# Column strips for the group norm of an SSM layer and for the query norm of an attention layer, with a wait put before some GpSimd splits

## The reference

```python
y = x * lax.rsqrt(jnp.mean(x * x, axis=-1, keepdims=True) + EPS)     # rmsnorm, of queries too (over 128)
y = y.reshape(b, L, D_INNER) * jax.nn.silu(z.astype(jnp.float32))
yg = y.reshape(b, L, SSM_GROUPS, D_INNER // SSM_GROUPS)
yg = yg * lax.rsqrt(jnp.mean(yg * yg, axis=-1, keepdims=True) + EPS) # the SSM norm
y = (yg.reshape(b, L, D_INNER) * norm_w.astype(jnp.float32)).astype(u.dtype)
return y @ w_out, new_conv, final.astype(u.dtype)
```

## Time and profile before

| | us |
|---|---|
| median of the runs (lowest to highest) | 1044.82 (1044.59 to 1044.83) |
| the profiled execution's own time | 1044.69 |
| its span, first to last instruction | 1042.9 |
| mean granted clock of TensorE | 0.990 of full speed |
| busy: PE, DVE, ACT, POOL | 994.5, 591.4, 462.8, 365.2 |

### The profile page before, as it was taken

The page is one execution under the profiler, slowest core; times in us unless marked ns, Lnnn a source line. Parts: engine busy times, 40 slices in busy tenths (PEclk is TensorE's granted clock), DMA queues, the critical chain, the costliest instruction groups (busy, mean ns, idle before and its releaser), DMA issues.

```text
span 1042.9 us, 18690 instructions
## 1 busy us (share of the span) xinstructions
PE 994.5 (95%) x7448; PEld 917.9 (88%) x7448; DVE 591.4 (57%) x1433; ACT 462.8 (44%) x811; POOL 365.2 (35%) x275
## 2 busy tenths in 40 slices
PE   8999999999999999999997899999999999999988
PEld 7998899979999799987996879998889987998867
DVE  5115431264214442255686587976879667896773
ACT  5324623257124633157535336343553436525553
POOL 4241133113332242311824144442354343542700
PEclk9999999999999999999999899999999999999989
DMA  6342121251232222200333643427242372426303
GB/s 195 103 149 84 56 84 50 59 180 41 82 107 100 81 82 84 85 21 1 85 104 117 167 136 92 149 60 221 76 154 82 104 205 61 136 82 190 108 11 97
DMA packets 144118, 106.37 MB, mean 102 GB/s; under 512 B 10258, under 2 KB 135364, under 8 KB 143840
## 3 DMA queue, kind: packets, MB, share of 16 engines
q1 hardware_dynamic: 115032, 92.24, 28.3%
q10 hardware_dynamic: 29000, 12.94, 4.8%
HBM read 92.44 MB, written 16.79 MB: 105 GB/s over the span
## 4 chain that ended last, share of the span: by engine, by line
PE 75%; DVE 14%; issue 4%; ACT 3%; POOL 2%; DMA 1%; ACTq 0%; SPq 0%; DVEq 0%; POOLq 0%
PE pp L1190 18%; PE pp L1192 17%; PE pp L1191 17%; DVE cv L1892 2%; PE pS L1294 2%; PE pS L1520 2%; PE pT_ L1499 1%; PE pO L1513 1%; PE pO L1509 1%; PE pO L1269 1%; DVE z L2034 1%; PE pO L1460 1%; ACT sm L792 1%; POOL w_lo_raw L603 1%; PE pO L1340 1%
## 5 line engine op out<-in xcount | busy, mean ns | idle before, releaser
L603 POOL TENSOR_TENSOR w_lo_buf<-w_raw_buf,w_hi_buf 128x512 fp32r<-128x512 f32 x214 | 287.6, 1375 | 522.2 <-ACT w_hi_buf L684 416.8
L1190 PE MATMUL pp<-h_hi,w_hi_buf 128*128 128x280 f32 (+1 forms) x1248 | 380.3, 305 | 5.7 <-DVE rb L1866 2.6
L1192 PE MATMUL pp<-h_hi,w_lo_buf 128*128 128x280 f32 (+1 forms) x1248 | 364.1, 292 | 0.0
L1191 PE MATMUL pp<-h_lo,w_hi_buf 128*128 128x280 f32 (+1 forms) x1248 | 363.5, 291 | 0.0
L1190 PEld LDWEIGHTS pp<-h_hi,w_hi_buf 128*128 128x128 f32 x1248 | 236.4, 189 | 16.8 <-issue 9.3
L1191 PEld LDWEIGHTS pp<-h_lo,w_hi_buf 128*128 128x128 f32 x1248 | 236.3, 189 | 4.6 <-issue 4.1
L1192 PEld LDWEIGHTS pp<-h_hi,w_lo_buf 128*128 128x128 f32 x1248 | 236.3, 189 | 0.0
L684 ACT ACTIVATE w_hi_buf<-w_raw_buf 128x2048 fp32r<-128x2048 f32 (+1 forms) x55 | 104.0, 1892 | 37.2 <-DMA w_raw_buf<-in_w_attn_in 16.0
L1678 DVE TENSOR_TENSOR x<-x,pp 128x272 f32<-128x272 f32 (+3 forms) x128 | 56.3, 440 | 79.2 <-PE pp L1192 78.4
L1190 PE MATMUL pp<-og_hi,w_hi_buf 128*128 128x280 f32 (+2 forms) x256 | 75.5, 295 | 2.5 <-DVE x L1678 1.3
L1192 PE MATMUL pp<-og_hi,w_lo_buf 128*128 128x280 f32 (+2 forms) x256 | 74.5, 291 | 0.0
(11 more groups left out here) (322 smaller groups left out, 1764.6 us busy)
## 6 DMA issues: line engine op xcount, KB each, us to landing
w_raw_buf<-in_w_attn_in SPq DMA_DIRECT2D x16, 1024.0 KB, 5.2
w_raw_buf<-in_w_ssm_in SPq DMA_DIRECT2D x16, 1024.0 KB, 5.5
w_raw_buf<-in_w_attn_out SPq DMA_DIRECT2D x8, 1024.0 KB, 6.3
s_in<-in_state_ssm SPq DMA_DIRECT2D x32, 256.0 KB, 4.2
out<-s_in SPq DMA_DIRECT2D x32, 256.0 KB, 3.1
seg<-a_scratch ACTq DMA_DIRECT2D x16, 512.0 KB, 4.3
w_raw_buf<-in_w_ssm_out SPq DMA_DIRECT2D x8, 1024.0 KB, 5.4
w_raw_buf<-in_w_attn_in SPq DMA_DIRECT2D x8, 512.0 KB, 6.3
```

The source lines that it names most:

```text
L603: ins = pool.tensor_tensor(low_buf(n)[:, piece], raw[n % RAW_SLOTS][:, piece], high_buf(n)[:, piece].bitcast(F32), ALU.subtract)
L1190: pe.matmul(dst, hi[:, k, cols], a_hi[:, k, tk], start=(k == 0), stop=False)
L1191: pe.matmul(dst, hi[:, k, cols], a_lo[:, k, tk], start=False, stop=False)
L1192: mm = pe.matmul(dst, lo[:, k, cols], a_hi[:, k, tk], start=False, stop=(k == depth - 1))
```

## The change

Three edits.

1. The query sums of all four heads are done in one place, after gate half (0, 0). Four matmuls with 32 weight columns each give the sample tokens' sums. For the prompt, ones[:, 0:32] are the weights and the squares are moved, one head to each strip of 32 output rows, in two halves of 280 columns. ACT takes the logarithm of the result (128 by 560) into `sq[0]`, PE turns it by five transposes (`turn_logs`, behind `scores(s, 0)`), and ACT takes Exp of every 32nd column. Two further square buffers are the key norm's `ksq` and `rk`.
2. In SSM groups 0 to 2 the sum over channels becomes `strips_y` (four matmuls into four strips of 32 rows of one bank), a copy of the strips by ACT, and `total_y` (one matmul with 128 by 128 ones; every strip holds its sum 32 times, hence the scale 1/(32 WIDTH)). `total_y` stands behind a half of a projection, and the final state's transposes move behind x half (1, 0).
3. POOL waits in the slab that follows gate (kv of the next group, or out of group 3): before its first piece until `soft_max` of unit 3 is done, before its third until that of unit 4 is.

```diff
-        sq = [at(f"sq{i}", [P, T]) for i in range(2)]
+        sq = [at(f"sq{i}", [P, T]) for i in range(2)] + [ksq, rk]
...
+                        if n in beside_soft and c in (0, m // 2):
+                            pool.wait_ge(soft_a, UNITS * beside_soft[n] + (5 if c else 4))
                         ins = pool.tensor_tensor(low_buf(n)[:, piece], raw[n % RAW_SLOTS][:, piece],
...
-                if 4 * s + h >= 2:
-                    act.wait_ge(ssq_done, 4 * s + h - 1)
-                act.activation(sq[h % 2][:, :], q[:, h, :], ACT.Square).then_inc(sq_ready, 1)
+                if h == 3:
+                    act.wait_ge(k_ready, s + 1)
+                act.activation(sq[h][:, :], q[:, h, :], ACT.Square).then_inc(sq_ready, 1)
...
-                act.wait_ge(ssq_done, 4 * s + 4)
-                link(act.activation(crow[:, 0:21], misc[:, 0:21], ACT.Ln, bias=eps[:, 1:2]))
-                act.activation(crow[:, 0:21], crow[:, 0:21], ACT.Exp, scale=-0.5).then_inc(c_ready, 1)
+                act.wait_ge(ssq_done, 2 * s + 1)
+                link(act.activation(crow[:, 20:21], misc[:, 16:17], ACT.Ln, bias=eps[:, 1:2]))
+                act.activation(crow[:, 20:21], crow[:, 20:21], ACT.Exp, scale=-0.5).then_inc(c_ready, 1)
+                act.wait_ge(ssq_done, 2 * s + 2)
+                act.activation(sq[0][:, :].rearrange("p (h t) -> p h t", h=2), pT_[:, :, 0:HALF], ACT.Ln,
+                               bias=eps[:, 1:2]).then_inc(logs_ready, 1)
+                act.wait_ge(turned, s + 1)
+                act.activation(crow[:, 0:20].rearrange("p (c h) -> p c h", h=HEADS),
+                               fT[:, 0:640].rearrange("p (c h r) -> p c h r", h=HEADS, r=32)[:, :, :, 0],
+                               ACT.Exp, scale=-0.5).then_inc(c_ready, 1)
...
+                    if g + 1 < GROUPS:
+                        act.wait_ge(strips_done, 2 * g + part + 1)
+                        act.activation(xc[:, 0, tk], pS[:, part, 0:n], ACT.Copy).then_inc(strips_ready, 1)
+                        act.wait_ge(ssy_done, 2 * g + part + 1)
+                        link(act.activation(v, pS[:, 1, 0:n], ACT.Ln, bias=eps[:, 0:1], scale=1.0 / (32 * WIDTH)))
...
+            def sum_q(s):
+
+                pe.wait_ge(sq_ready, 4 * s + 4)
+                if s:
+                    pe.wait_ge(o_ready, UNITS * s)
+                for h in range(HEADS):
+                    mm = pe.matmul(misc[32 * h:32 * h + 32, 16:17], sq[h][:, PROMPT:T], ones[:, 0:1],
+                                   start=True, stop=True)
+                mm.then_inc(ssq_done, 1)
+                pe.wait_ge(tok_ready, s + 1)
+                for half in range(2):
+                    for h in range(HEADS):
+                        mm = pe.matmul(pT_[32 * h:32 * h + 32, half, 0:HALF], ones[:, 0:32],
+                                       sq[h][:, half * HALF:(half + 1) * HALF], start=True, stop=True)
+                mm.then_inc(ssq_done, 1)
+
+            def turn_logs(s):
+
+                pe.wait_ge(logs_ready, s + 1)
+                for i, c in enumerate((1, 2, 3, 4, 0)):
+                    mm = pe.transpose(fT[:, i * P:(i + 1) * P], sq[0][:, COL[c]:COL[c] + P], ident)
+                mm.then_inc(turned, 1)
...
-                sum_q(s, 0)
                 tile_of("q", s, 2)
-                sum_q(s, 1)
                 tile_of("q", s, 3)
-                sum_q(s, 2)
                 project("gate", s, 0, 0)
-                sum_q(s, 3)
+                sum_q(s)
                 scores(s, 0)
+                turn_logs(s)
                 project("gate", s, 0, 1)
...
+            def strips_y(g, part):
+                tk = part_of(g, part)
+                pe.wait_ge(xw_done, UNITS * (g + 1))
+                if part:
+                    pe.wait_ge(rg_ready, 2 * g + 1)
+                pe.wait_ge(sqy_ready, 8 * g + 4 * part + HEADS)
+                for t in range(HEADS):
+                    mm = pe.matmul(pS[32 * t:32 * t + 32, part, 0:tk.stop - tk.start], ones[:, 0:32], xc[:, t, tk],
+                                   start=True, stop=True)
+                mm.then_inc(strips_done, 1)
+
+            def total_y(g, part):
+                tk = part_of(g, part)
+                pe.wait_ge(strips_ready, 2 * g + part + 1)
+                pe.matmul(pS[:, 1, 0:tk.stop - tk.start], ones[:, :], xc[:, 0, tk],
+                          start=True, stop=True).then_inc(ssy_done, 1)
...
                 project("x", s, 0, 0)
                 if g:
-                    sum_y(g - 1, 1)
+                    strips_y(g - 1, 1)
                 project("x", s, 0, 1)
                 if g:
+                    total_y(g - 1, 1)
+                project("x", s, 1, 0)
+                if g:
                     final_state(g - 1)
-                tile_of("x", s, 1)
+                project("x", s, 1, 1)
...
-                    sum_y(g, 0)
+                    strips_y(g, 0)
                     project("bc", s + 1, 1, 1)
+                    total_y(g, 0)
```

More of the change, by code:

```diff
@@ L361, in build @@
         sq_ready, ssq_done, c_ready = sem("sq_ready"), sem("ssq_done"), sem("c_ready")
+        logs_ready, turned = sem("logs_ready"), sem("turned")
+        strips_done, strips_ready = sem("strips_done"), sem("strips_ready")
         s_done, soft_a, exp_done, p_ready = sem("s_done"), sem("soft_a"), sem("exp_done"), sem("p_ready")
@@ L417, in colsum @@
         def colsum(c):
-            return 16 if c == 5 else 17 if c == 0 else (c - 1) * 4
+            return 20 if c == 5 else 16 if c == 0 else (c - 1) * 4
         def fill_pairs(g):
@@ L591, in _ @@
             done = [0]
+            beside_soft = {slab_no[("kv", s + 1, 0)] if s + 1 < GROUPS else slab_no[("out", s, 0)]: s
+                           for s in range(GROUPS)}
             def split_lo(upto):
@@ L1112, in scale_y @@
                 def scale_y(part):
-                    act.wait_ge(ssy_done, 2 * g + part + 1)
                     tk = part_of(g, part)
                     v, n = scale_of(g)[:, tk], tk.stop - tk.start
-                    link(act.activation(v, pS[:, part, 0:n], ACT.Ln, bias=eps[:, 0:1], scale=1.0 / WIDTH))
+                    if g + 1 < GROUPS:
[3 more added lines that the diff above has]
+                        link(act.activation(v, pS[:, 1, 0:n], ACT.Ln, bias=eps[:, 0:1], scale=1.0 / (32 * WIDTH)))
+                    else:
+                        act.wait_ge(ssy_done, 2 * g + part + 1)
+                        link(act.activation(v, pS[:, part, 0:n], ACT.Ln, bias=eps[:, 0:1], scale=1.0 / WIDTH))
                     act.activation(v, v, ACT.Exp, scale=-0.5).then_inc(rg_ready, 1)
@@ L1288, in scores @@
                         pe.matmul(pS[:, i, :], lhs, kcT[:, 4 * i:4 * i + 4, :], start=True, stop=True)
-                    pe.wait_ge(c_ready, s + 1)
+                    pe.wait_ge(c_ready, 2 * s + 1)
                     pe.matmul(misc[:, 32:64], lhs, kq[:, PROMPT:T], start=True, stop=True).then_inc(s_done, 1)
@@ L1304, in transposes @@
                 if u == 0:
-                    pe.wait_ge(tok_ready, s + 1)
+                    pe.wait_ge(c_ready, 2 * s + 2)
                 p = sm[v % 2]
@@ L1537, in _ @@
                 if g:
-                    pe.wait_ge(rg_ready, 2 * g - 1)
+                    pe.wait_ge(strips_ready, 2 * g - 1)
                 else:
@@ L1692, in soft_max @@
                 dve.wait_ge(s_done, v + 1)
-                dve.wait_ge(c_ready, s + 1)
+                dve.wait_ge(c_ready, 2 * s + (2 if u else 1))
                 if v >= 2:
```

## The result

| | us |
|---|---|
| kernel after, median of four runs (lowest to highest) | 1029.7 (1028.3 to 1031.7) |
| kernel before, in the same comparison | 1044.7 (1043.9 to 1044.8) |
| ratio after to before, 95% interval | 0.9859 (0.9838 to 0.9881) |
| profiled execution of after, its span | 1028.36, 1026.6 |

The gain is 15 us by the medians and 16.3 us between the two profiled executions (1044.69 to 1028.36); 18.9 was forecast. The median lies in the range, but two of the three edits brought more than forecast and the third lost where a small gain was forecast.

The account below looks back on a forecast made before the run. PE carries 75% of the chain of waits, DVE 14%. Savings of 6.8 (GpSimd pieces), 9.3 and 1.3 (query sums, groups 1 to 3 and 0) and 1.5 (SSM norm) sum to 18.9 us, from 1044.69 to 1025.8; range 1021 to 1032.5.

Parts of the forecast that it names:

- the 1.7 to 1.9 us of PE's waiting: Softmax unit 3, each attention group: of 3.1 us DVE time saved, 1.7 to 1.9 are PE's; 6.8 us in four groups.
- margin of tenths: Moved GpSimd pieces: first two end near 100.4, `normalise` starts at about 100.6; both fits have a few tenths to spare.
- rival A: Softmax units 3 and 4: moved pieces collide with `normalise` again, gaining 2.4 instead of 6.8 us; 1030.2 us, chance 0.10.
- 0.94 + 0.24 + 0.3: Query sums' added PE work: 0.94 us two stripped halves of 280 columns, 0.24 loads and gaps, 0.3 one-column sample passes.
- Rival B: Query sums and SSM norm: strips do not run abreast with 280 or 384 columns; 1041.8 us, chance 0.04.
- The wait for gate's remainder (0.4): Attention group 0: PE reaches the gate slab before POOL's remainder is done, costing 0.4 us of the query-sum saving.
- the clock: Group 0, after PE's longer stall: TensorE may stay longer at its lower clock, worth 0 to 1.5 us.
- Part 0: SSM norm, first part: strips and total save 1.0 us of PE, but PE then waits 0.9 before x half (0, 0).
- the 0.90 us for GpSimd: SSM boundary: PE arrives early at x half (0, 0) and waits 0.9 us for POOL's remainder of slab x0.
- rival D: SSM boundaries: output slabs load late behind the moved final state, PE waits beyond 5.0 us slack; 1048.6 us, chance 0.03.
- Rival C: SSM stretch: DVE-POOL contention hits other instructions, 1 us a boundary, and clock costs 1.5 in group 0; 1031.8 us, chance 0.10.

Follow-up runs that it names:

- pieces_only: Only the GpSimd waits before two pieces of the slab that follows gate, on the kernel before: 1037.07 us, ratio 0.9925.
- one_gate: `pieces_only` with one GpSimd wait in place of two, so all four pieces start after unit 3's maxima: 1039.61 us, ratio 0.9945.
- query_only: Only the query sums in strips, done in one place, on the kernel before: 1033.57 us, ratio 0.9894.
- norm_only: Only the SSM norm by strips, copy and total, with the final state one half later, on the kernel before: 1050.85 us, ratio 1.0055.
- no_norm: Query sums in strips and the GpSimd waits together, without the SSM norm change, on the kernel before: 1025.12 us, ratio 0.9804.
- load_gate: Full change plus first output slab loaded before the final-state wait, and GpSimd waiting before the second until y part 0's remainders are done: 1021.79 us.
- move_only: `no_norm` with only the final state's transposes moved behind x half (1, 0), sums staying four full matmuls: 1037.40 us, ratio 0.9937.

## Why the prediction was right, and where it was wrong

**Edit 3, right in mechanism, somewhat small.** 6.8 us forecast, 7.6 by the end of attention in `pieces_only` and 8.2 by the medians. The step was the 1.7 to 1.9 us of PE's waiting a group, of which I took the lower end; it was 1.9. The margin of tenths was real (pieces end 0.1 us after `normalise` begins), and rival A, which lives on it, did not come. Of its two collisions one was forced in `one_gate`: 2.5 us by the medians, 1.6 by the end of attention, where A had 4.4 for both, so its price was about right. But it had the small instructions held, and what was held is the four multiplications. That the excess of `pieces_only` over 7.6 is real is not shown.

**Edit 1, the sum mis-sized.** 3.1 us a group forecast, 3.6 measured, so the added work cost 5.24 - 3.6 = 1.6 us of PE instead of 2.13. The rows say where: from the first one-column pass to the scores it is 72.02 - 70.87 = 1.15 us, for which I had 0.94 + 0.24 + 0.3 = 1.48. The one-column passes in strips cost about 0.1, not 0.3 (less than the 0.2 that I had as the least), and of the 0.24 for loads and gaps only 0.1 shows. The five transposes cost 0.50 (2.46 us from the scores to the next half of gate in after, 1.96 before), for which I had 0.55 + 0.1. Rival B is dead: the strips run abreast at 280 and at 384 columns (0.85 us, 0.9 forecast), and the drain that the Trainium skill (TensorEngine Tiling, Key Properties) warns of does not show beside these times. Group 0 was forecast to keep 1.3; in `query_only` GpSimd's split of unit 3 comes 2.1 us earlier (93.90 against 95.97), which is about 3.6 - 1.36 with nothing off. The wait for gate's remainder (0.4) did not come, and the clock cost nothing more: PE's stall grows from 1.61 to 2.82 us, as worked out, but the low clock behind it lasts no longer. The rows are `query_only` and then before; the stretch from 52 to 54 was not in the earlier trace rows.

```profile
52.00:54.00 2.00, 1.09 (x5) 1.12 (x6) 0.00 (x0) 0.00 (x0) 0.65 (x1) 0.66 0.45 141
54.00:56.00 2.00, 2.00 (x10) 2.00 (x10) 0.00 (x0) 0.00 (x0) 0.00 (x0) 0.50 0.78 242
...
52.00:54.00 2.00, 1.12 (x5) 1.15 (x6) 0.00 (x0) 0.00 (x0) 0.78 (x1) 0.60 0.58 191
```

**Edit 2, wrong.** Forecast +1.5 us, bounds -3 and +5. Measured -5.6 alone and -5.1 beside the others, outside the bounds. (In the profiled executions alone, the part behind attention is 3.8 us longer in `norm_only` than in before and 3.7 longer in after than in `no_norm`, which is outside the bound of -3 too.) Part 0 went as worked out, down to the 0.90 us for GpSimd. The step that failed is the last of that section, "the final state moves behind x half (1, 0) ... and ACT and SP wait for it", and its companion in rival D. I computed the delay of the output slab rightly (2.8 us, measured 2.9), and then asked only when PE needs the slab (5.0 us of slack). I did not ask what DVE does in the 6 us in which GpSimd splits it. I had used just that question for the softmax, at the earlier trace rows, and the rows needed were at hand: pieces until 662.89, `low_y` at 666.69, 3.8 us on. The move and the 1.1 us by which DVE came sooner use those up. Rival C had the mechanism (contention falls on other instructions) at 1 us a boundary. It is 2.1 us of waiting at each, then the clock, and its total of 1031.8 owed some of its nearness to gains that came out larger elsewhere.

**The sum.** 8.2 + 11.7 - 5.6 = 14.3 against 6.8 + 10.6 + 1.5 = 18.9. Errors of +2.5 and -7.1 partly cancel. That the median lies in the range is luck to that extent: the 17.4 forecast for edits 1 and 3 and the -5.6 of edit 2 would have made 1032.9 us, just outside.

**Behind the attention layer.** In `query_only` attention ends 13.0 us earlier and the kernel 11.3 (span 1031.6). Some 1.7 us go after the attention layer. The trace places most of it in the last group, where PE is busy throughout at a low granted clock:

```profile
954.00:956.00 2.00, 2.00 (x11) 1.77 (x10) 0.88 (x2) 2.00 (x2) 2.00 (x3) 0.50 0.84 248
956.00:958.00 2.00, 2.00 (x13) 2.00 (x13) 1.71 (x1) 0.70 (x1) 2.00 (x2) 0.71 0.09 21
```

At full speed the work of these 4 us would take about 2.4, an estimate from their clocks, so 1.6 are lost. The last group of `no_norm` has the same (0.50 and 0.69 from 946 to 950) and is longer than that of before (162.0 against 160.4 us from group 2's last decay to the end); before and `pieces_only` stay at 1.00 at that place. What lets the clock fall in one kernel and not in the other is not shown.

## What to carry to other kernels

A transfer or a step that is moved later must be followed through each engine that handles it, not only at its consumer: here the slab had 5 us of slack for PE and 3.8 us until its GpSimd pieces met DVE's remainders, on which PE waits. A wait for GpSimd ahead of a few instructions that are on the path (edit 3, `load_gate`) gained 4 to 8 us, while filling GpSimd's idle time lost 3 to 5, since DVE was busy there. Strips of 32 columns paid in the query sums (3.6 us a group); in the SSM norm their gain stayed within the intervals.

## What the runs showed of the hardware

GpSimd's pieces stretch most DVE work whose operands all lie in SBUF, and are stretched themselves. Four subtractions of 128 by 384 take 1.96 us alone and 5.74 under pieces, and a split of four pieces takes 5.00 us alone and 6.91 beside them, so neither side is free. That agrees with the Trainium skill (SBUF — State Buffer, SBUF: two separate sides), by which the port pair is held for a whole instruction. Two kinds of instruction were not stretched: the masked copy, which reads PSUM (0.42 us under the pieces), and the reciprocal of 128 by 4 (0.18 us inside a piece of `one_gate`), though it lies in SBUF altogether. What I had not expected is how far it reaches: the same four subtractions took 1.96, 3.04, 4.67 or 5.74 us in kernels that differ by a microsecond or two in when the pieces start.

Waits of 0.9 us in a row, with three matmuls between them, were followed by a granted clock of 0.53 to 0.81 over 4 to 8 us at some boundaries, and by none at another with nearly the same waits. A chain of short waits can so cost more than their sum: in the trace of `move_only`, with 9.7 us of them, the part behind attention is 10.9 us longer than in `no_norm`, although PE's other waits for DVE there shrank by some 4 us.
